# Two-pass head sums and a re-timed group tail in a hybrid RWKV-7 / forgetting-attention decoder layer

## What is computed

```python
u = rmsnorm(h, attn_norm_g) @ w_in                     # one projection, two head groups read it
# RWKV-7 half: 16 heads x 64
u = u + (token_shift(u) - u) * mu                      # r, k, v and three small parts are split from it
kk = kk / max(norm(kk), 1e-12)                         # per head
bonus = sum(rh * kh * r_k, axis=-1) * vh               # per head, over its 64 features
y = (groupnorm(scan(r, decay, k, v, kk, a)) + bonus) * g
# forgetting attention half: 16 heads x 64
q, k = rmsnorm(heads(q), q_norm_g), rmsnorm(heads(k), k_norm_g)     # per head, over its 64 features
o = softmax(q k^T / 8 + c_q - c_k, causal) v
h = h + concat(y, o) @ w_out
h = h + (silu(hn @ w_gate) * (hn @ w_up)) @ w_down     # hn = rmsnorm(h)
h = h + sigmoid(rmsnorm(h) @ ple_gate_w + b) * rmsnorm(p @ ple_proj)
```

## Time and profile before

| | |
|---|---|
| median of 3 runs | 2797.43 us (2796.32 to 2798.48) |
| the profiled execution | 2798.53 us, of which the span from first to last instruction 2796.7 us |
| PE busy | 2712.5 us, 97% of the span |
| DVE, ACT, POOL busy | 1151.0, 1008.7, 217.1 us |
| DMA queues' packets, share of 16 engines | 27.4% (q1, the weights) |
| mean granted TensorE clock | 0.991 of full speed |

### The profile page before, as it was taken

How to read it: one execution, slowest core, us unless ns; L and a number is a source line. 1 busy time by engine, 2 the same in 40 slices (tenths; PEclk the granted TensorE clock), 3 DMA queues, 4 the chain that set the end, 5 groups by cost and what they waited for, 6 DMA issues and landing times.

```text
span 2796.7 us, 41084 instructions
## 1 busy us (share of the span) xinstructions
PE 2712.5 (97%) x15562; PEld 2155.5 (77%) x15562; DVE 1151.0 (41%) x1693; ACT 1008.7 (36%) x1435; POOL 217.1 (8%) x348
## 2 busy tenths in 40 slices
PE   7999999998999999999999999999999999999998
PEld 5776766676766678888888888888888888888787
DVE  6642652652553434433333333333333333334443
ACT  5424533543544433533222333223332222234421
POOL 2000210110120110200000000000000000011300
PEclk9999999999999999999999999999999999999999
DMA  4221221221212433322233222332222322223232
GB/s 165 76 84 57 68 84 50 69 78 52 72 62 75 139 103 102 107 94 95 86 95 111 96 92 87 96 109 97 94 91 89 109 97 97 92 83 109 97 118 79
DMA packets 108120, 255.91 MB, mean 92 GB/s; under 512 B 35272, under 2 KB 37832, under 8 KB 108008
## 3 DMA queue, kind: packets, MB, share of 16 engines
q1 hardware_dynamic: 105904, 247.10, 27.4%
q0 software_dynamic: 2112, 7.34, 0.7%
HBM read 245.43 MB, written 8.98 MB: 91 GB/s over the span
## 4 chain that ended last, share of the span: by engine, by line
issue 59%; PE 29%; DVE 5%; ACT 4%; DMA 2%; SPq 1%; POOL 1%; DVEq 0%; POOLq 0%; ACTq 0%
PE bank L302 7%; PE bank L299 7%; PE bank L303 7%; PE bank L338 4%; PE bank L460 1%; PE bank L489 1%; ACT w_hi L287 1%; PE bank L476 1%; DMA x_raw<-xT 1%; SPq L1264 0%; DVE acc_x L1632 0%; DVE w_lo L294 0%; SPq L1250 0%; DMA solved_scratch<-solved 0%; PE bank L438 0%
## 5 line engine op out<-in xcount | busy, mean ns | idle before, releaser
L294 DVE TENSOR_TENSOR w_lo<-raw,w_hi 128x1024 fp32r<-128x1024 f32 (+1 forms) x484 | 543.6, 1126 | 942.9 <-ACT w_hi L287 938.0
L287 ACT ACTIVATE w_hi<-raw 128x1024 fp32r<-128x1024 f32 (+1 forms) x484 | 471.2, 975 | 988.1 <-PE bank L303 950.9
L299 PE MATMUL bank<-hn_hi,w_hi 128*128 128x512 f32 x1664 | 648.1, 389 | 0.0
L303 PE MATMUL bank<-hn_hi,w_lo 128*128 128x512 f32 x1664 | 647.3, 389 | 0.0
L302 PE MATMUL bank<-hn_lo,w_hi 128*128 128x512 f32 x1664 | 647.3, 389 | 0.0
L299 PE MATMUL bank<-in_hi,w_hi 128*128 128x512 f32 x1088 | 467.5, 430 | 49.1 <-DMA VT_t<-solved_scratch 11.3
L302 PE MATMUL bank<-in_lo,w_hi 128*128 128x512 f32 x1088 | 443.8, 408 | 0.0
L303 PE MATMUL bank<-in_hi,w_lo 128*128 128x512 f32 x1088 | 429.4, 395 | 0.0
L302 PEld LDWEIGHTS bank<-hn_lo,w_hi 128*128 128x128 f32 x1664 | 312.4, 188 | 65.6 <-issue 0.5
L303 PEld LDWEIGHTS bank<-hn_hi,w_lo 128*128 128x128 f32 x1664 | 312.4, 188 | 65.1
L299 PEld LDWEIGHTS bank<-hn_hi,w_hi 128*128 128x128 f32 x1664 | 312.4, 188 | 64.6 <-issue 0.5
(11 more groups left out here) (233 smaller groups left out, 2116.1 us busy)
## 6 DMA issues: line engine op xcount, KB each, us to landing
raw<-w_gu SPq DMA_DIRECT2D x176, 512.0 KB, 3.4
raw<-w_mix SPq DMA_DIRECT2D x116, 512.0 KB, 3.6
raw<-w_down SPq DMA_DIRECT2D x64, 384.0 KB, 3.1
raw<-w_down SPq DMA_DIRECT2D x64, 320.0 KB, 2.9
raw<-ple_gate SPq DMA_DIRECT2D x32, 512.0 KB, 3.5
raw<-w_mix SPq DMA_DIRECT2D x28, 384.0 KB, 3.3
x_raw<-xT SPq DMA_DIRECT2D x4, 1024.0 KB, 11.5
h_t<-xT SPq DMA_DIRECT2D x4, 1024.0 KB, 6.4
```

Of the source, the lines that this page charges most:

```text
L287: nc.scalar.activation(w_hi[:, ring_slots(par2, half), 0:cols[half]], raw[:, half, 0:cols[half]], ACT.Copy).then_inc(hi_ready, 1)
L294: nc.vector.tensor_tensor(w_lo[:, s, 0:cols[half]], raw[:, half, 0:cols[half]], w_hi[:, s, 0:cols[half]].bitcast(F32), ALU.subtract).then_ ...
L299: nc.tensor.matmul(out, w_h, x_hi, start=start, stop=False, skip_group_check=True)
L303: return nc.tensor.matmul(out, w_l, x_hi, start=False, stop=stop, skip_group_check=True)
```

## The change

- The block matrix of ones is rounded once to fp32r (`blocks_r`). The eight bonus sums and the sixteen sums of squares of q and k are made of two parts: ACT copies `t1`, rounded, to a `high` tile; DVE takes the rest to `t1_low`, in place over `t1`; PE makes two fp32r products (`pe_block_sum`). The high part lies over `t2` or `bonus`.
- The bonus sum moves from step 4 to step 11 of slabs 2 and 5; its high copy stands at step 5, the low part at step 6, the copy of the sum at step 12.
- The four norms' sums move from step 4 to steps 8, 6, 6, 5; Ln from step 5 to 9, 7, 8, 7; Exp to 9, 7, 10, 9; the scaling by DVE from step 6 to 10, 8, 11, 10. On ACT and DVE the chain's work of a step now stands ahead of the norm's work of that step.
- In slab 6 shift and mixing of the second value tile and its product with the bonus move from the slab's start to step 9, behind the masked copies; PE's turn of the values moves from step 4 to 13.
- The bursts X and D and the chain start one slot later.

```diff
-X_SLOTS, D_SLOTS = (42, 47), (44, 49)
-CHAIN_SLOT, CHAIN_STEP = 52, 5
+X_SLOTS, D_SLOTS = (43, 48), (45, 50)
+CHAIN_SLOT, CHAIN_STEP = 53, 5
+MIX_AT = 9
+BONUS_AT = 11
+FOX_SUM_AT, FOX_LN_AT, FOX_EXP_AT, FOX_QK_AT = (8, 6, 6, 5), (9, 7, 8, 7), (9, 7, 10, 9), (10, 8, 11, 10)
...
+    def pe_block_sum(high, low):
+        nc.tensor.matmul(aux[:], blocks_r[:], high, start=True, stop=False)
+        return nc.tensor.matmul(aux[:], blocks_r[:], low, start=False, stop=True)
...
-        if kind == 2 and kt == 4:
-            pe.wait_ge(S("rk_ready"), f + 1)
+        if kind == 2 and kt == BONUS_AT:
+            pe.wait_ge(S("rk_low_ready"), f + 1)
             pe.wait_ge(S("k_sum_ready"), f + 1)
-            nc.tensor.matmul(aux[:], const(C_BLK), t1[:], start=True, stop=True).then_inc(S("bonus_done"), 1)
+            pe_block_sum(bonus_high[:, ft, :], t1_low[:]).then_inc(S("bonus_done"), 1)
...
-        if kind == 2 and kt == 5:
+        if kind == 2 and kt == BONUS_AT - 6:
+            act.wait_ge(S("rk_ready"), f + 1)
+            nc.scalar.activation(bonus_high[:, ft, :], t1[:], ACT.Copy).then_inc(S("rk_high_ready"), 1)
+        if kind == 2 and kt == BONUS_AT + 1:
             act.wait_ge(S("bonus_done"), f + 1)
             nc.scalar.activation(bonus[:, ft, :], aux[:], ACT.Copy).then_inc(S("bonus_ready"), 1)
...
             nc.scalar.activation(t1[:], u_t[:, 1:SEQ + 1], ACT.Square).then_inc(S("fox_square_ready"), 1)
-        if 0 <= c < 4 and kt == 5:
+            nc.scalar.activation(t2_high[:], t1[:], ACT.Copy).then_inc(S("fox_square_high_ready"), 1)
+        if 0 <= c < 4 and kt == FOX_LN_AT[c]:
             nc.scalar.activation(t2[:], aux[:], ACT.Ln, scale=1.0 / HD, bias=cb(CB_RMS)
+        if 0 <= c < 4 and kt == FOX_EXP_AT[c]:
             nc.scalar.activation(t2[:], t2[:], ACT.Exp, scale=-0.5).then_inc(S("fox_rstd_ready"), 1)
...
+        if s == 6 and kt == MIX_AT:
+            dve_shift(dve, LORA_SLABS + GROUP_SLABS * g + 5)
+            dve_mix_values(dve, g, 1)
+        if 0 <= c < 4 and kt == 3:
+            low_part(t2_high[:]).then_inc(S("fox_square_low_ready"), 1)
...
-                            act_fox_prep(act, s, kt, g)
                             act_recurrence(act, s, kt, g)
+                            act_fox_prep(act, s, kt, g)
...
+                            dve_recurrence(dve, s, kt, g)
                             dve_fox_prep(dve, s, kt, g)
-                            dve_recurrence(dve, s, kt, g)
```

More of the change, by code:

```diff
@@ L90 @@
 C_COL = C_I16 + SB * SB
+SIZES = {"low": (SEQ,), "high": (SEQ,), "high_pair": (2, SEQ)}
 PAR = {}
@@ L248, in layer @@
     small = sb("small", [P, 64])
+    blocks_r = sb("blocks_r", [P, P], F32R)
+    t1_low, t2_high = rounded("low", "t1"), rounded("high", "t2")
+    bonus_high = rounded("high_pair", "bonus")
     psum = [nc.alloc_psum_tensor(f"bank{i}", [P, SEQ], F32) for i in range(8)]
@@ L392, in pe_fox_prep @@
     def pe_fox_prep(pe, s, kt, g):
-        if kt != 4 or s < 6:
-            return
-        if s == 6:
+        if s == 6 and kt == MIX_AT + 4:
             yield from pe_values(pe, 2 * g + 1)
-            return
         c = s - 7
-        if c < 4:
-            pe.wait_ge(S("fox_square_ready"), 4 * g + c + 1)
+        if 0 <= c < 4 and kt == FOX_SUM_AT[c]:
+            pe.wait_ge(S("fox_square_low_ready"), 4 * g + c + 1)
             if c == 0:
@@ L405, in pe_fox_prep @@
                 pe.wait_ge(S("fox_rstd_ready"), 4 * g + c)
-            nc.tensor.matmul(aux[:], const(C_BLK), t1[:], start=True, stop=True).then_inc(S("fox_sum_done"), 1)
-        else:
+            pe_block_sum(t2_high[:], t1_low[:]).then_inc(S("fox_sum_done"), 1)
+        if c == 4 and kt == 4:
             pe.wait_ge(S("fox_rstd_ready"), 4 * g + 4)
@@ L691, in act_fox_prep @@
     def act_fox_prep(act, s, kt, g):
-        if s == 6 and kt == 5:
+        if s == 6 and kt == MIX_AT + 5:
             act_values(act, g, 1)
@@ L836, in dve_arrival_rwkv, with dve_mix_values, low_part @@
             nc.vector.tensor_tensor(AR[:, ft, 1, :], AR[:, ft, 1, :], d_t[:], ALU.mult).then_inc(S("R_ready"), 1)
-        if kind == 2:
-            nc.vector.scalar_tensor_tensor(out=t2[:], in0=t1[:], scalar=gp_col(MU_V), in1=u_t[:, 1:SEQ + 1],
-                                           op0=ALU.mult, op1=ALU.add).then_inc(S("v_mixed"), 1)
-            dve.wait_ge(S("v_mixed"), f + 1)
-            dve.wait_ge(S("bonus_ready"), f + 1)
-            nc.vector.tensor_tensor(bonus[:, ft, :], bonus[:, ft, :], t2[:], ALU.mult).then_inc(S("bonus_v_ready"), 1)
+        if kind == 2 and ft == 0:
+            dve_mix_values(dve, g, 0)
+    def dve_mix_values(dve, g, ft):
+        f = 2 * g + ft
+        if ft == 1:
+            dve.wait_ge(S("shift_ready"), LORA_SLABS + 3 * f + 3)
+        nc.vector.scalar_tensor_tensor(out=t2[:], in0=t1[:], scalar=g_par[:, ft, MU_V:MU_V + 1],
+                                       in1=u_t[:, 1:SEQ + 1], op0=ALU.mult, op1=ALU.add).then_inc(S("v_mixed"), 1)
+        dve.wait_ge(S("v_mixed"), f + 1)
+        dve.wait_ge(S("bonus_ready"), f + 1)
+        nc.vector.tensor_tensor(bonus[:, ft, :], bonus[:, ft, :], t2[:], ALU.mult).then_inc(S("bonus_v_ready"), 1)
+    def low_part(high):
+        return nc.vector.tensor_tensor(t1_low[:], t1[:], high.bitcast(F32), ALU.subtract)
     def dve_rwkv_prep(dve, s, kt, g):
@@ L864, in dve_rwkv_prep @@
                                     ).then_inc(S("st_exponent_ready"), 1)
+        if kind == 2 and kt == BONUS_AT - 5:
+            dve.wait_ge(S("rk_high_ready"), f + 1)
+            low_part(bonus_high[:, ft, :]).then_inc(S("rk_low_ready"), 1)
         if kind == 1 and kt == 5:
@@ L1494, in _ @@
                 act_arrival_lora(act, n - 1)
+            act.wait_ge(S("consts_landed"), 32)
+            nc.scalar.activation(blocks_r[:], const(C_BLK), ACT.Copy).then_inc(S("blocks_rounded"), 1)
             def group(g, gp):
```

24 lines of the change are left out of this document (18 added, 6 removed).

## The result

| | before | after |
|---|---|---|
| median of 5 runs, us | 2797.43 (2796.32 to 2802.32) | 2783.55 (2780.46 to 2784.79) |
| ratio, 95% interval | 1 | 0.9942 (0.9931 to 0.9952) |
| span of the profiled execution, us | 2796.7 | 2781.7 |
| half clock in the four groups of the profiled execution, us | 37.4 | 34.0 |

The change makes the kernel 13.9 us faster, 0.6%. The forecast was 2758.5, 25.0 us less, and the time is 6.6 us above the upper end of its range. The last row of the table adds up the stretches of 3.4 or 6.8 us at a granted clock of 0.50 between 100 and 1020 us of the span: the change took eight of them away and seven others came.

A forecast was written before the change was run, and what follows sets the result against it. PE, busy 97% of the span, was taken as the bound, through single waits, fp32 sums and half clock. From 2798.53, -26.5 (waits and sums) and -12.5 (clock) gave 2759.5, 2758.5 as median; range 2743 to 2777.

The forecast's parts named there:

- slab 9: PE's wait of 1.91 us for U becomes 1.07 (R0 0.48, U 0.59); with the sum -1.27 per group.
- Sums: Two fp32r products (0.45 us) replace one fp32 sum (0.89): 0.43 less for each of 24 sums, 10.3 us.
- Slab 6 to the first X burst: Solved blocks land sooner, so X starts sooner: -2.6 us each in groups 2 to 4, -2.9 in the first.
- First group, slabs 2 and 5: Bonus sum without attention: a wait of 0.94 us replaces 1.94; with the sum -1.42, twice.
- Slab 10: Chain waits of 1.10 us (0.34 + 0.76) become 1.07; with the sum -0.45 per group.
- Slab 11: PE's wait for the state, 1.87 us, becomes 0.5: -1.38 per group.
- Slab 5: Groups 2 to 4: the 2.03 us wait for r·k goes, one of 2.7 for POOL comes; net +0.25 each.
- The clock in slab 5: Half clock behind the new 2.7 us wait: 2 chances in 3 of 1.7 us, thrice, +3.5 us.
- the old falls: Half clock at the first X burst (2.78 us in three groups, 1.62 in the first) and slab 11 goes: 16.0 us.
- the first (the clock falls as before): Rival: the clock still falls, with waits of 1.4 and 1.2 us in slab 8: 2774 us; chance 0.20.
- the fourth: Rival: new copies cost more, slab 8's low part or Ln ahead of R0 taking longer: 2793 to 2802; chance 0.07.
- its own bounds of 2750 to 2768: Forecast's spread: slab 5's clock 0 to 5 us, waits of slabs 8 to 10 0.4 either way; chance 0.52.

The follow-up runs named there:

- Experiment 1: Changed kernel with the first chunk's new state ahead of the second half slab on DVE in slab 9, step 8: 2762.15 us.
- experiments 2 and 3: Each on the changed kernel: X, D and chain one slot back, 2774.32 us; slab 9's logarithm one step later (9 instead of 8), 2769.62 us.
- experiment 9: Kernel of 2750.04 us (state step first, slab 5's last scaling by DVE, early copies), with single fp32 products for slabs 7 to 10's sums: 2752.59 us.
- Experiment 8: Kernel of Experiment 1 (2762.15 us) with the second value tile's mixing back at slab 6's start and the turn back at step 4: 2765.99 us.
- experiment 5: Kernel of Experiment 1 (2762.15 us) with the bonus sum of slabs 2 and 5 put back as one fp32 product at step 4: 2763.83 us.

## Why the prediction was wrong

**The step that failed is slab 9.** The prediction followed ACT's queue there: the logarithm and the rounding ahead of R0, the exponential ahead of U, waits of 0.48 and 0.59, together 1.07. It didn't follow DVE's, on which the first state of slab 9 had a wait of nothing in the sum. With the chain's start moved from slot 52 to 53, the first state step moved from step 7 to step 8 of slab 9, where the half slab stands ahead of it on DVE. The new order on ACT made that half slab late. The prediction named exactly this pair (half slab behind rounding, state behind half slab) in slab 11, as the wait that the moved chain gets rid of, and didn't ask which other state step would now fall into a step with a half slab. The first one did, in every group: 3.8 to 3.9 us instead of 1.07, and a clock that fell behind each of them. Experiment 1 undoes this alone, and gives back 21.4 of the 25.0 us; experiments 2 and 3, which take the state step and the logarithm out of the chain, agree with it.

**The other terms, one by one.**

- Sums: 0.46 for the pair, 0.45 said; 0.88 for the single one against 0.89 (experiment 9). Right.
- Slab 6 to the first X burst: -2.6 said for groups 2 to 4. From DVE's first scaling in slab 6 (L793, L815) to the end of the wait for `VT_t` lie 40.12, 41.15, 41.03 and 40.72 us in the four groups before and 39.28, 39.20, 39.20 and 38.72 after, with one step of 0.68 more in it: -1.52, -2.63, -2.51 and -2.68. Right in groups 2 to 4; in the first group, where -2.9 was said, only -1.5. In the third group the solve ended 29.8 us behind the start of slab 6, as said; the waits on the way were 1.03 for slab 8's low part (1.4 said; 1.39 in the first group) and 1.18 for `VT_t` (1.2 said). Experiment 8 bears out the reason given, the late mixing: without it the wait for the rows ends 3.8 us later, all four groups together.
- First group, slabs 2 and 5: the waits are 0.84 and 0.77, 0.94 said. Right.
- Slab 10: R and U wait 0.33 each, 0.66 in all, where 1.07 was said. Slab 11: 0.33 for the state, 0.5 said, and no fall of the clock. Better than said. In slab 9 too R and U wait only 0.33 each once the state is out of the way (experiment 1).
- Slab 5: the wait for POOL came, as forecast, but 3.3 us long instead of 2.7. What failed here is the step that POOL would be as quick as before. The scaling took 2.19 instead of 1.67 with DVE's low part beside it, and 1.67 again without (experiment 5). The Trainium skill, "SBUF — State Buffer", section "Who interferes with whom", says that a VectorE instruction with two inputs in SBUF contends with a GpSimd instruction that reads SBUF; the low part is such a subtraction, and the 0.52 us agree with it. The half slabs are such subtractions too, and beside them the scaling took 1.67 us where it takes 0.70 alone; the prediction carried these 1.67 us over as POOL's own time.
- The clock in slab 5: two chances in three of 1.7 us were counted, 3.5 us in all. In the profile it fell in all three groups, for 3.4 to 6.8 us, 13.6 in all, part of it inside the wait.

**The clock as a whole.** That the old falls go was right: none of the eight is left. Their price of 16.0 us was not measured by itself. But seven new ones came behind the two new waits, and of the rivals the first (the clock falls as before) comes nearest in kind, at other places than it said; the fourth named Ln's stay ahead of R0, and Ln did hold PE up, but by way of the rounding, the half slab and the state. With the slip in slab 9 mended, the change gives 2762.15: 3.7 us above the forecast and within its own bounds of 2750 to 2768. That this is so close is in part luck: slab 5 costs more than said, in wait and clock, and the first group's way to X gains less, while R, U and the state in slabs 9 to 11 wait some 4 us less than said. The sign and the existence of the wait in slab 5 were right; one queue at one place was not read.

## What to carry to other kernels

When a change moves the slots of one periodic schedule against another, list for every engine which of its steps now fall together, and look at each of these pairs anew; to follow the one queue in which the known wait was is not enough. Put small work that another engine waits for ahead of large work that has time, even if the large work stood first for good reasons elsewhere. And a short wait ahead of a fixed landing is not worth removing: it joins the next one, and the longer wait can cost the clock.
